# Copying the caches of a hybrid decoder step in pieces of six rows instead of three

## The reference

```python
h = rms_norm(x, norm_g)
proj = jnp.einsum('btd,de->bte', h, w_in)
...
kk = jnp.concatenate([k_buf, k], axis=1)
vv = jnp.concatenate([v_buf, v], axis=1)
o = dilated_attention(q, kk, vv, k_buf.shape[1])
...
new_k = kk[:, -n_keep:]
new_v = vv[:, -n_keep:]
y = jnp.einsum('bte,ed->btd', jnp.concatenate([ya, yb, yc], axis=-1), w_out)
return x + y, new_conv, new_pool, new_k, new_v
```

## Time and profile before

| | before |
|---|---|
| median of three runs | 440.1 us (437.45 to 445.49) |
| the profiled execution, its own time | 439.78 us |
| its span, first to last instruction | 438.0 us |
| PE busy | 347.8 us (79%) |
| DVE busy | 232.1 us (53%) |
| ACT busy | 103.2 us (24%) |
| POOL busy | 38.4 us (9%) |
| moved by DMA | 158.06 MB, mean 361 GB/s |
| DRAM read and written | 154.90 and 104.42 MB |
| mean granted PE clock | 0.926 of full speed |

### The profile page before, as it was taken

The page is one execution under the profiler, slowest core; times in us unless marked ns, Lnnn a source line. Parts: engine busy times, 40 slices in busy tenths (PEclk is TensorE's granted clock), DMA queues, the critical chain, the costliest instruction groups (busy, mean ns, idle before and its releaser), DMA issues.

```text
span 438.0 us, 4497 instructions
## 1 busy us (share of the span) xinstructions
PE 347.8 (79%) x1552; PEld 269.3 (61%) x1552; DVE 232.1 (53%) x522; ACT 103.2 (24%) x243; POOL 38.4 (9%) x70
## 2 busy tenths in 40 slices
PE   1799999947897999997999998498979999960000
PEld 1688888835675656886888887367755568840000
DVE  0626997998677643104278979985865421100000
ACT  4101145223342131102011533143321401130000
POOL 0014101100101011010011001110100111110000
PEclk9999999996999899999999999969989999995555
DMA  8999999999999999999999999999999999999941
GB/s 296 360 368 298 375 365 395 414 389 409 418 414 390 336 342 368 424 417 390 414 394 405 393 415 349 380 407 418 412 364 326 329 329 326 332 333 379 330 182 49
DMA packets 47301, 158.06 MB, mean 361 GB/s; under 512 B 3861, under 2 KB 16351, under 8 KB 46703
## 3 DMA queue, kind: packets, MB, share of 16 engines
q0 software_dynamic: 22592, 100.62, 62.7%
q1 hardware_dynamic: 15508, 33.85, 21.2%
q10 hardware_dynamic: 9178, 23.31, 14.2%
HBM read 154.90 MB, written 104.42 MB: 592 GB/s over the span
## 4 chain that ended last, share of the span: by engine, by line
PE 58%; DVE 16%; DMA 8%; ACT 3%; issue 2%; SPq 1%; ACTq 0%; DVEq 0%
PE pj L543 28%; PE pj L682 13%; DMA kv<-in_cache_v_win 7%; PE psc L614 6%; DVE kv L1058 4%; DVE ssc L1061 4%; DVE yc L1118 3%; PE ptr L469 2%; PE ps L491 2%; DMA cst<-in_const 1%; SPq L373 1%; PE psc L469 1%; PE ps L665 1%; PE prt L555 1%; PE ps L553 1%
## 5 line engine op out<-in xcount | busy, mean ns | idle before, releaser
L543 PE MATMUL pj<-hT,w 128*128 128x264 f32 x800 | 188.8, 394 | 3.0 <-DVE hT L980 3.0
L543 PEld LDWEIGHTS pj<-hT,w 128*128 128x128 f32 x800 | 152.9, 194 | 32.6 <-issue 7.0
L1118 DVE SCALAR_TENSOR_TENSOR yc<-u_ext,par,yc 128x256 f32<-128x256 f32 x180 | 76.2, 480 | 2.8 <-DVE u_smp L1008 0.6
L682 PE MATMUL pj<-mix,w 128*128 128x264 f32 x256 | 59.3, 386 | 0.0
L682 PEld LDWEIGHTS pj<-mix,w 128*128 128x128 f32 x256 | 48.5, 190 | 8.2
L1188 DVE TENSOR_TENSOR xT<-xT,pj 128x264 f32<-128x264 f32 x16 | 6.9, 429 | 53.6 <-PE pj L682 53.6
L461 POOL DMA_DIRECT2D out<-in_cache_v_win x32 | 18.6, 581 | 186.4 <-issue 186.4
L461 POOL DMA_DIRECT2D out<-in_cache_k_win x32 | 18.6, 584 | 160.5 <-issue 129.4
L614 PE MATMUL psc<-kv,spm 128*48 128x384 f32 x80 | 27.5, 496 | 0.4 <-DMA kv<-in_cache_v_win 0.4
L803 ACT ACTIVATE ex<-pj 128x264 f32<-128x264 f32 x22 | 8.6, 390 | 75.1 <-PE pj L543 60.9
L909 ACT ACTIVATE hT<-xT 128x264 f32<-128x264 f32 x16 | 6.8, 423 | 66.1 <-DVE xT L1188 66.1
(11 more groups left out here) (169 smaller groups left out, 331.5 us busy)
## 6 DMA issues: line engine op xcount, KB each, us to landing
out<-in_cache_k_win POOLq DMA_DIRECT2D x32, 1512.0 KB, 72.1
out<-in_cache_v_win POOLq DMA_DIRECT2D x32, 1512.0 KB, 68.9
w<-in_w_out ACTq DMA_DIRECT2D x2, 4096.0 KB, 28.9
w<-in_w_in ACTq DMA_DIRECT2D x1, 4608.0 KB, 29.0
kv<-in_cache_k_win SPq DMA_DIRECT2D x32, 144.0 KB, 28.4
w<-in_w_in ACTq DMA_DIRECT2D x3, 1536.0 KB, 27.5
kv<-in_cache_v_win SPq DMA_DIRECT2D x32, 144.0 KB, 20.7
w<-in_w_in SPq DMA_DIRECT2D x1, 4608.0 KB, 28.5
```

The lines of the kernel that those rows point to most:

```text
L543: last = nc.tensor.matmul(pj[n % RING][:, 0:T], wbuf[buf][:, k, col:col + P], hT[:, k, :], start=(k == 0), stop=(k == KD - 1))
L682: last = nc.tensor.matmul(pj[n % RING][:, 0:T], w1[:, k, m * P:(m + 1) * P], mix[:, k, :], start=(k == 0), stop=(k == KD - 1))
L1118: last = V.scalar_tensor_tensor(out=yc[:, t, 0:SEQ], in0=x_w, scalar=par[:, ROW_CW + w * CT + t:ROW_CW + w * CT + t + 1], in1=yc[:, t, 0:S ...
```

## The change

A copy now takes a whole sample's 2016 rows (`COPIES`), not half of it, and a piece is six rows, 9216 B. So there are 32 issues for 64, of 3024 KB each. The number of pieces in one issue stays 21 for each of the 16 DMA engines, the total of bytes and the two issues for the last 31 rows stay too. Each of the 16 semaphores is used twice and no longer four times.

```diff
-HALF_ROWS, PIECE_ROWS = 1008, 3
-HALVES = [(kind, s, h) for kind in ("k", "v") for s in range(NS) for h in range(2)]
+COPY_ROWS, PIECE_ROWS = 2016, 6
+COPIES = [(kind, s) for kind in ("k", "v") for s in range(NS)]
...
-                sp.wait_ge(half_out[i], 16 * DEPTH * len(HALVES) // IN_FLIGHT)
+                sp.wait_ge(half_out[i], 16 * DEPTH * len(COPIES) // IN_FLIGHT)
...
-                for i, (kind, s, h) in enumerate(HALVES):
+                for i, (kind, s) in enumerate(COPIES):
                     cache, out = (ins["cache_k_win"], o_k_s) if kind == "k" else (ins["cache_v_win"], o_v_s)
-                    a, b = h * HALF_ROWS, (h + 1) * HALF_ROWS
-                    dst = out[l, s, a:b].rearrange("(c e r) h d -> c e (r h d)", c=16, r=PIECE_ROWS)
-                    src = cache[l, s, a + 1:b + 1].rearrange("(c e r) h d -> c e (r h d)", c=16, r=PIECE_ROWS)
+                    dst = out[l, s, 0:COPY_ROWS].rearrange("(c e r) h d -> c e (r h d)", c=16, r=PIECE_ROWS)
+                    src = cache[l, s, 1:COPY_ROWS + 1].rearrange("(c e r) h d -> c e (r h d)", c=16, r=PIECE_ROWS)
                     pool.dma_start(dst, src, max_dma_last_dim=PIECE_ROWS * C_ATT * 4).then_inc(half_out[i % IN_FLIGHT], 16)
```

More of the change, by code:

```diff
@@ L170 @@
 ACT_SCHEDULE.insert(ACT_SCHEDULE.index(("proj", PIDX[("b_gate", 0)])), "ln2")
-HALF_ROWS, PIECE_ROWS = 1008, 3
-HALVES = [(kind, s, h) for kind in ("k", "v") for s in range(NS) for h in range(2)]
+COPY_ROWS, PIECE_ROWS = 2016, 6
+COPIES = [(kind, s) for kind in ("k", "v") for s in range(NS)]
 IN_FLIGHT = 16
-assert len(HALVES) % IN_FLIGHT == 0
+assert len(COPIES) % IN_FLIGHT == 0
 XROUNDS = 5
@@ L455, in _ @@
             for l in reversed(range(DEPTH)):
-                for i, (kind, s, h) in enumerate(HALVES):
+                for i, (kind, s) in enumerate(COPIES):
                     cache, out = (ins["cache_k_win"], o_k_s) if kind == "k" else (ins["cache_v_win"], o_v_s)
-                    a, b = h * HALF_ROWS, (h + 1) * HALF_ROWS
-                    dst = out[l, s, a:b].rearrange("(c e r) h d -> c e (r h d)", c=16, r=PIECE_ROWS)
-                    src = cache[l, s, a + 1:b + 1].rearrange("(c e r) h d -> c e (r h d)", c=16, r=PIECE_ROWS)
+                    dst = out[l, s, 0:COPY_ROWS].rearrange("(c e r) h d -> c e (r h d)", c=16, r=PIECE_ROWS)
+                    src = cache[l, s, 1:COPY_ROWS + 1].rearrange("(c e r) h d -> c e (r h d)", c=16, r=PIECE_ROWS)
                     pool.dma_start(dst, src, max_dma_last_dim=PIECE_ROWS * C_ATT * 4).then_inc(half_out[i % IN_FLIGHT], 16)
             for cache, out in ((ins["cache_k_win"], o_k_s), (ins["cache_v_win"], o_v_s)):
-                pool.dma_start(out.rearrange("l s t h d -> (l s) (t h d)")[:, 2 * HALF_ROWS * C_ATT:(PAST - 1) * C_ATT],
-                               cache.rearrange("l s t h d -> (l s) (t h d)")[:, (2 * HALF_ROWS + 1) * C_ATT:]).then_inc(bulk_out, 16)
+                pool.dma_start(out.rearrange("l s t h d -> (l s) (t h d)")[:, COPY_ROWS * C_ATT:(PAST - 1) * C_ATT],
+                               cache.rearrange("l s t h d -> (l s) (t h d)")[:, (COPY_ROWS + 1) * C_ATT:]).then_inc(bulk_out, 16)
         @block.tensor
```

## The result

The changed kernel takes **499.94 us** (median of four runs, 497.64 to 502.1) for 440.7 us of the kernel before: a ratio of 1.137, 95% interval 1.128 to 1.146. It is slower by 59 us, inside the range that was given (450 to 515), 14 us above the predicted time. The profiled execution took 497.64 us, its span 495.8 us.

A forecast was written before the change was run, and what follows sets the result against it. Full DMA engines serving queues piece by piece bound the kernel, with copies setting the end. Lateness 25 + 24 + 28 + 12 = 89 moves the compute's end from 392.15 to 481.2; with output and overhead 486 us, range 450 to 515.

The forecast's parts named there:

- One piece a turn, whatever its size: DMA engines serve the queues in turn, one piece each; the copies' piece size sets how long a load waits.
- Copies are bound by bytes: DRAM traffic, 604 to 655 GB/s with copies counted twice, was taken as the nearer limit.
- Fewer issues are worth nothing: At GpSimd's issues: POOL waits for ring room either way and no one waits for POOL; worth nothing.
- 42 us are hidden: At the end of the span: copies set the end, so the compute has about 42 us to spare.
- Keys of layer 0: Gather of keys, layer 0: large pieces +3, small pieces x1.7 or +23, less 0.7 spare; 25 us late (22 to 32).
- Keys of layer 1: `a_in` and the keys' gather, layer 1: 39 to 56, taken 48, less 19.9 cover; 28 more (19 to 36).
- Values of layer 0: Gather of values, layer 0: small pieces x1.6 or +25, less 1.6 spare; 24 more us late (17 to 35).
- up to 10: `b_in`, ahead of layer 0's values on SP's queue and behind the late keys, could add this; left to the range.
- Values of layer 1: Gather of values, layer 1: small pieces partly run without copies, landing at 418, not 406; 12 more (0 to 25).
- The end of the copies near 410: All copies and loads beside them at 0.60 to 0.655 MB/us end at 403 to 437; 410 was taken.
- upper bounds: Turn length if DRAM limits: grows with traffic, copies counted twice; 1.86 for copies with one 1536 B stream.
- lower ones: Turn length if engines limit: grows with bytes moved in it; 1.75 for copies with one 1536 B stream.

The follow-up runs named there:

- the two runs that part the piece from the issue: Against the kernel before: whole samples per issue in three-row pieces, ratio 0.9996; half samples per issue in seven-row pieces, ratio 1.183.
- first eight samples: Kernel before with six-row pieces, a whole sample per issue, for the first 8 of 32 samples' copies only: 445.25 us, ratio 1.0048.
- two rows: Changed kernel's whole-sample issues with two-row pieces asked for, 3072 B, in place of six rows: 445.3 us, ratio 1.006 to the kernel before.
- first sixteen: Kernel before with six-row pieces, a whole sample per issue, for the first 16 of 32 samples' copies: 469.06 us, ratio 1.058.

## Why the prediction was right, point by point

| station | before | after | added lateness | predicted |
|---|---|---|---|---|
| keys of layer 0 used | 77.62 | 104.04 | 26.4 | 25 |
| values of layer 0 used | 144.09 | 207.63 | 37.1 | 24 |
| keys of layer 1 used | 262.06 | 357.10 | 31.5 | 28 |
| values of layer 1 used | 329.13 | 428.48 | 4.3 | 12 |
| chain of compute ends | 392.15 | 493.05 | 1.6 | 0 |
| sum | | | 100.9 | 89 |

*One piece a turn, whatever its size.* Right, and shown: the counts from 70 to 90 us stay equal with twice the size, the records follow each other queue by queue, and the two runs that part the piece from the issue put the cost in time on the piece.

*Copies are bound by bytes.* Right: 327 GB/s with six rows, 328 with three. *Fewer issues are worth nothing.* Right in the time, ratio 0.9996; up to 7 us of lateness may be theirs.

*42 us are hidden.* Right: a chain 42 to 43 us late leaves the time within 1% (first eight samples; two rows), and one that is 77 us late brings 34 (first sixteen, the profiled execution: 473.89 us for 439.78 us of the profiled one before).

*Keys of layer 0.* 26.4 for 25, but as the sum of two errors. The eight large pieces were to land 3 us later and landed at 44.1 for 44.0, in part because the copies started 4 us later in this execution; the small pieces took 59.9 us for 33.0, x1.81, near the upper bound of 1.86 and not the 1.7 taken. That they cancel is luck.

*Keys of layer 1.* The stretch from the issue of `a_in` to the last landing was 78.3 us and became 126.7 (230.31 to 314.89 + 42.13): x1.62, 48 us more, as taken; less 19.8 of spare time it is 28.6. The other 2.9 of the 31.5 us came in before it, in PE's matmuls on the values (below).

*Values of layer 0.* This is the term that failed in size: "24 more", and it was 37.1. The last of the eight large pieces' issues and its landing, issue 9, and the landing of `b_in`, first in the kernel before, then in the changed one:

```profile
92.31 0.59 SPq L373 DMA_DIRECT2D kv<-in_cache_v_win  x1
kv<-in_cache_v_win SPq DMA_DIRECT2D x1, 192.0 KB, 10.9
...
118.49 0.59 SPq L373 DMA_DIRECT2D kv<-in_cache_v_win  x1
kv<-in_cache_v_win SPq DMA_DIRECT2D x1, 192.0 KB, 24.7
126.65 0.58 SPq L373 DMA_DIRECT2D kv<-in_cache_v_win  x1
w<-in_w_in SPq DMA_DIRECT2D x1, 2048.0 KB, 69.9
```

In the kernel before the large pieces had landed 3.0 us after issue 9 (103.2 for 100.23). In the changed one it was 16.5 us (143.2 for 126.65), because `b_in`, issued at 65.72 behind the late keys, stood ahead of them on SP's queue and landed only at 135.6. That is 13.5 us; the prediction had left it out of the sum, with "up to 10" in the range. The small pieces behind them took 64.3 us for 39.4: 25 more, x1.63, as taken. Together 38.5, less the 1.4 us of spare time that this used up: 37.1. Moving `b_in` off this queue brought the large pieces' landing back to 3.7 us after issue 9 and saved 10.7 us in all. With six rows for the first eight samples, whose six-row copies are through by 134 us, before the small pieces run, these took 39.3 us as in the kernel before, and all 8 us of the values' further lateness are this queue ahead of them.

*Values of layer 1.* 4.3 for 12, again two errors that cancel. `b_in` was there too, landed at 389.2, and put the large pieces' landing 17.1 us after issue 9 (1.9 before): 15 us that the prediction had not. But this moved the small pieces to where the copies end, and they took 31.6 us for 42.5: from 410 to 423 us GpSimd's queue has 76 pieces and SP's 1017. The end of the copies near 410 was taken rightly. In the run with six rows for all but the first nine, where the copies go on, the same gather shows both parts in full: 17.5 us from the queue ahead and 22.0 in the small pieces, x1.52.

*What sets a turn's length.* The prediction's upper bounds assume that DRAM does, the lower ones that the engines do. The DRAM traffic in the changed kernel's 70 to 90 us is (2 x 5.50 + 0.97 + 0.84) MB in 20 us, 640 GB/s, near the 655 of copies alone. That fits DRAM; but the engines are full there too, and no run parts the two.

*What I left out.* In the changed kernel PE stands idle for 37.9 us before the values of layer 0, and its granted clock is at its lower level, half speed, by then: 0.50 from 200 to 208 us. The first 16 matmuls of L613 then take 8.08 us for 5.33 with the clock at full speed; those of layer 1 take 6.89. These are the 2.9 us in the keys of layer 1 and the 1.6 in the table's last row. And the profiled execution before was an early one, as its second weight load, from before any copy, landed at 31.3 us, and not at 35.3 as in the changed one or at 33.8 to 36.5 as in the other runs that start the copies there; by the run with six rows for the last eight samples some 6 of the 101 us are owed to that and not to the change.

*The number.* The lateness came out 12 us over the sum, and the median stands 2.3 us above the profiled execution where 0.3 was taken: 14 us in all. That 486 is as near as this is partly luck, since the 13 to 15 us of `b_in` in each layer, left out twice, were made good once by the copies' end.

## What to carry to other kernels

Before making a background copy's pieces larger, look at who else is on the DMA engines: with pieces served in turn, the size of the piece is the background's share, and each foreground load of many small pieces is stretched by it. Count also what stands ahead of a load on its own queue: a load that had landed in time before may not any more, and then its whole rest is in the way. Read the spare time between the compute's end and the copies' end first; what stays below it is free, and can be spent on starting the background earlier. A larger piece is worth a try only where a stretch without loads shows that copies are not bound by bytes, and here none did.

## What the runs showed that I had not expected

Pieces of 3072 B did not reach the engines as such: 16960 records with a mean of 6 KB, for 32,256 asked; those of 4608, 9216 and 10752 B did. And an issue of ACT can hold its computing: 18.3 and 33.5 us in two issues while loads issued before them were still under way, against 0.4 us else. The changed kernel has a small case of it (5.25 us at 326.68), and SP's issues there stretch to 4 to 6 us each, which is why a third of its chain of waits is put down to SP's line L373; that it is for the same reason is likely and not shown.
